# Three block seams and one loop order of a hybrid decoder step: two end-of-block transfer waits moved into the next block, the delta preparation's vector order turned round, and the first state-space quarter reordered

## The reference, cut to what matters

```
hn  = rms_norm(x) * (1 + sc1) + sh1                # modulation from c through w_ada
qkv, z, beta, alpha, u = split(hn @ w_in)
q, k, v = silu(short causal conv(qkv)); q, k normalised per head (4 heads of 128)
o   = gated delta rule(q, k, v, exp(g), beta)      # in chunks: triangular solve, then a scan
y   = S5(u)                                        # 32 groups of 16 channels, 64 complex states:
                                                   # x_t = Lbar x_{t-1} + Bbar u_t ; y = Re(C x) + D u
y   = gelu(y); y = y * sigmoid(y @ glu_w + glu_b)
x   = x + gt1 * (concat(norm(o)*silu(z), norm(y)) @ w_out)
x   = x + gt2 * moe(rms_norm(x)*(1+sc2)+sh2)       # 16 experts, top 2 within the best group of 4
out = rms_norm(x)
```

## Time and profile before

| | |
|---|---|
| median of three runs | 1240.59 us (1237.02 to 1242.99) |
| the profiled execution's own time | 1234.19 us |
| its span, first to last instruction | 1232.6 us, 15219 instructions |
| mean granted TensorE clock | 0.942 of full speed |
| TensorE matmul busy | 1077.2 us (87%) |
| VectorE busy | 553.9 us (45%) |
| ScalarE busy | 310.5 us (25%) |
| GpSimd busy | 217.5 us (18%) |
| block 1 | start to 382.2 us |
| block 2 | 382.2 to 514.8 us |
| block 3 | 514.8 to 629.9 us |
| block 4 | 629.9 us to the end |

### The profile page before, as it was taken

The page is one execution under the profiler, slowest core; times in us unless marked ns, Lnnn a source line. Parts: engine busy times, 40 slices in busy tenths (PEclk is TensorE's granted clock), DMA queues, the critical chain, the costliest instruction groups (busy, mean ns, idle before and its releaser), DMA issues. The chain is left out here.

```text
span 1232.6 us, 15219 instructions
## 1 busy us (share of the span) xinstructions
PE 1077.2 (87%) x5092; PEld 645.0 (52%) x5093; DVE 553.9 (45%) x1290; ACT 310.5 (25%) x703; POOL 217.5 (18%) x368
## 2 busy tenths in 40 slices
PE   4899999899996789499988899991999999889876
PEld 4466666445865677478763444441444444444332
DVE  3234446774355555598904424664311111111128
ACT  5122121135113443332233333321011111011033
POOL 0000000384413335100110000122210111001060
PEclk8999999999998899898988999995999999999888
DMA  9595170120016000575553100017586664788273
GB/s 345 152 292 217 68 272 1 69 103 35 14 27 139 2 1 2 164 265 188 185 193 134 69 35 19 35 46 176 167 274 223 220 223 159 266 309 287 102 290 139
DMA packets 128048, 182.02 MB, mean 148 GB/s; under 512 B 37725, under 2 KB 81490, under 8 KB 127982
## 3 DMA queue, kind: packets, MB, share of 16 engines
q1 hardware_dynamic: 116988, 147.03, 36.2%
q0 software_dynamic: 7376, 21.59, 5.4%
q10 hardware_dynamic: 3626, 12.64, 2.5%
HBM read 131.69 MB, written 48.47 MB: 146 GB/s over the span
## 5 line engine op out<-in xcount | busy, mean ns | idle before, releaser
L2163 PE MATMUL bank<-w_out,H 128*128 (+1 forms) x384 | 172.0, 601 | 10.2 <-DMA w_out<-in_w_up 5.5
L368 PE MATMUL bank<-hT,w_ring 128*128 128x344 f32 x576 | 169.7, 456 | 3.8 <-ACT hT L552 3.8
L368 PEld LDWEIGHTS bank<-hT,w_ring 128*128 128x128 f32 x576 | 109.9, 192 | 62.0 <-issue 5.4
L2163 PEld LDWEIGHTS bank<-w_out,H 128*128 128x128 f32 x384 | 72.4, 192 | 107.3 <-issue 105.4
L453 PE MATMUL bank<-w_ring,hT 128*128 128x512 f32 x256 | 114.7, 605 | 4.3 <-ACT qkvT L580 4.3
L2481 PE MATMUL bank<-w_out,hT 128*128 128x512 f32 x256 | 116.8, 601 | 0.5 <-DVE hT L1940 0.5
L2230 DVE TENSOR_TENSOR H<-H,bank 128x256 f32<-128x256 f32 x24 | 10.1, 421 | 238.2 <-ACT H L2199 238.2
L2145 PE MATMUL bank<-y1T,H 128*128 (+1 forms) x192 | 91.1, 618 | 10.7 <-DVE H L2239 7.8
L453 PEld LDWEIGHTS bank<-w_ring,hT 128*128 128x128 f32 x256 | 64.2, 255 | 50.5 <-issue 32.1
L2481 PEld LDWEIGHTS bank<-w_out,hT 128*128 128x128 f32 x256 | 46.3, 190 | 49.8 <-issue 47.2
L2145 PEld LDWEIGHTS bank<-y1T,H 128*128 128x128 f32 x192 | 35.4, 194 | 52.1 <-issue 51.7
(11 more groups left out here) (556 smaller groups left out, 1742.7 us busy)
## 6 DMA issues: line engine op xcount, KB each, us to landing
ys_d<-ZO SPq DMA_DIRECT2D x18, 1024.0 KB, 13.0
y1T<-in_w_down SPq DMA_DIRECT2D x16, 1024.0 KB, 5.4
w_out<-in_w_gate SPq DMA_DIRECT2D x16, 1024.0 KB, 8.6
w_out<-in_w_up SPq DMA_DIRECT2D x16, 1024.0 KB, 11.4
ys_d<-H ACTq DMA_DIRECT2D x24, 512.0 KB, 5.1
w_ring<-in_w_in SPq DMA_DIRECT2D x4, 2048.0 KB, 8.2
y1T<-in_w_ada SPq DMA_DIRECT2D x4, 2048.0 KB, 8.7
hT<-in_w_ada SPq DMA_DIRECT2D x4, 2048.0 KB, 13.0
```

What stands on the lines that cost most here:

```text
L368: mm = t.matmul(ps[3 * (m % 2) + s][:, 0:SEG], w_ring[:, q % 2, k, (m % 4) * P:(m % 4 + 1) * P], hT[:, k, s * SEG:(s + 1) * SEG], start=(k ...
L2163: mm = t.matmul(ps[2 + p][:, :], xT[p][:, k, :], wgu[:, bass.ds(buf, 1), k, :].rearrange("p o n -> p (o n)"), start=(k == 0), stop=(k == K ...
```

## The change

Four edits, which do not touch what is computed. The wait for the t_d and tt_d writes goes from the end of block 1 to the head of SyncE's stream in block 2. VectorE's preparation loop issues decay(c+1) behind at(c). The wait for the S5 state writes goes from the end of block 3 into VectorE's stream of block 4, behind its wait for glu_w and glu_b. And in the first quarter of block 3, GpSimd clears Vq first under a name of its own; TensorE turns V before it waits for anything, and waits for "clear" only at the modulation products; VectorE begins with table W, copies Vq behind it, and forms X0r and X0i between the tables CL and CS.

```diff
 # block 1, SyncE
                 sp.dma_start(tt_d.rearrange("p (i j) -> p i j", i=BL), Lx).then_inc(t_out, 16)
-                sp.wait_ge(t_out, 32)
 # block 2, SyncE
             def _(sp):
+                sp.wait_ge(t_out, 32)
                 for dst, src in ((Yd, tt_d), (Xd, t_d)):
 # block 2, VectorE
                 for c in range(NT):
                     b = c % 2
-                    if c + 1 < NT:
-                        decay(c + 1)
                     act.wait(v, f"egb{c}")
                     dve.did(v.tensor_copy(egl[:, c, :], egb[:, :, P - 1]), f"egl{c}")
 ...
                     dve.did(v.tensor_tensor(at_t(c), heads(ps[2 + c % 2][:, :]), D1[:, b], ALU.mult), f"at{c}")
+                    if c + 1 < NT:
+                        decay(c + 1)
 # block 3, SyncE
-                sp.wait_ge(s5_out, 64)
 # block 3, GpSimd
             def _(g):
+                pool.did(g.memset(Vq[:, :, :, :], 0.0), "Vq")
                 pool.did(g.memset(cP4[:, :, :], 0.0))
 ...
                 pool.did(g.memset(TT[:, :, :, :], 0.0))
-                pool.did(g.memset(Vq[:, :, :, :], 0.0))
                 pool.did(g.memset(zs[:, :, 0:1], 0.0), "clear")
 # block 3, TensorE (turn_inputs is split into turn_rows and turn_decode)
-                pool.wait(t, "clear")
+                turn_rows(0)
                 for q in range(4):
 ...
                     if q == 0:
-                        turn_inputs(0)
+                        turn_decode(0)
 ...
                     dve.wait(t, f"K{q}")
+                    if q == 0:
+                        pool.wait(t, "clear")
                     for c in (2 * q, 2 * q + 1):
 # block 3, VectorE
-                tt(X0r[:, :, :], X0[:, :, :], bc(LC[:, 0, :, 1], [P, GROUPS, DEC]), ALU.mult)
-                tt(X0i[:, :, :], X0[:, :, :], bc(LC[:, 1, :, 1], [P, GROUPS, DEC]), ALU.mult, "x0")
+                def decode_inputs(q):
+                    if q > 0:
+                        pe.wait(v, f"U{q - 1}")
+                    else:
+                        pool.wait(v, "Vq")
 ...
                     table(W[:, :, :, :], Wt[:, :, 0:LAGS, :], LB, Bb[:, gs, :], B2[:, gs, :], LAGS, ALU.add, f"W{q}")
+                    if q == 0:
+                        decode_inputs(0)
 ...
                     table(CL, Wt[:, :, :, :], LC, q1, q2, LAGS + 1, ALU.add, f"CL{q}")
+                    if q == 0:
+                        dve.did(v.tensor_tensor(X0r[:, :, :], X0[:, :, :], bc(LC[:, 0, :, 1], [P, GROUPS, DEC]), ALU.mult))
+                        dve.did(v.tensor_tensor(X0i[:, :, :], X0[:, :, :], bc(LC[:, 1, :, 1], [P, GROUPS, DEC]), ALU.mult), "x0")
                     table(CS, Wt[:, :, 0:LAGS, :], LC, q2, q1, LAGS, ALU.subtract, None, first=1)
-                decode_inputs(0)
                 tables(0)
 # block 4, VectorE
             v.wait_ge(g_land, 32)
+            v.wait_ge(s5_out, 64)
             for i in range(10):
```

More of the change, by code:

```diff
@@ L1616, in turn_inputs, with turn_rows, turn_decode @@
                         dve.wait(t, f"rot{q - 1}_1")
+                    turn_rows(q)
+                    turn_decode(q)
+                def turn_rows(q):
                     for x in range(NG):
-                        mm = t.transpose(ps[2 + x // 4][:, (x % 4) * P:(x % 4 + 1) * P],
-                                         V[:, q * NG + x].rearrange("p j c -> p (j c)"), ident[:, :])
+                        t.transpose(ps[2 + x // 4][:, (x % 4) * P:(x % 4 + 1) * P],
+                                    V[:, q * NG + x].rearrange("p j c -> p (j c)"), ident[:, :])
+                def turn_decode(q):
                     dve.wait(t, f"Vq{q}")
@@ L1755, in tt @@
                     dve.did(v.tensor_tensor(out, x, y, op), name)
-                tt(X0r[:, :, :], X0[:, :, :], bc(LC[:, 0, :, 1], [P, GROUPS, DEC]), ALU.mult)
-                tt(X0i[:, :, :], X0[:, :, :], bc(LC[:, 1, :, 1], [P, GROUPS, DEC]), ALU.mult, "x0")
+                def decode_inputs(q):
[3 more added lines that the diff above has]
+                        pool.wait(v, "Vq")
+                    dve.did(v.tensor_copy(Vq[:, :, LAGS - 1, :], Vd[:, q * P:(q + 1) * P].rearrange("b (g c) -> b g c", c=CH)), f"Vq{q}")
                 def tables(q):
```

## The result

The changed kernel takes 1219.75 us in the median of four runs (1217.23 to 1224.40), beside 1238.80 for the kernel before on the same chip: ratio 0.9842, interval 0.9810 to 0.9874. Six more runs in a later batch gave 0.9852 (0.9814 to 0.9890). The profiled execution took 1217.45 us, forecast 1217.2; its span fell from 1232.6 to 1215.6 us, by 17.0.

The account below looks back on a forecast made before the run. Bounds named: SyncE's write waits at block ends, a loop of waits in the preparation, and block 3's first quarter. Gains 2.6 + 9.4 + 1.2 + 3.8 = 17.0 us took 1240.6 to 1223.6, range 1214 to 1236.

Parts of the forecast that it names:

- A: Seam of blocks 1 and 2: SyncE's tt_d write wait leaves the block end, gaining 2.6 us (bounds 0 and 2.7).
- rival 1: Block ends wait for SyncE's outstanding writes anyway, so moving both write waits gives 0: 1227.4 us; chance 0.09.
- B: Delta preparation in block 2: decay(c+1) behind at(c) shortens a chunk from 4.23 to 2.94 us, gaining 9.4 (bounds 7, 10.6).
- The loop named in the prediction: Preparation: waits through R, D1, vb, the turn of v, kv, Gb and next R set the 4.23 us chunk.
- rival 2: Preparation's two-chunk loop closes in one chunk: 5.88 us instead of 4.23, losing 11.6, total 1244.6; chance 0.06.
- rival 3: Preparation: D1(c) meets GpSimd's qg(c) every chunk, period 4.2 us again, no gain there, time 1233; chance 0.05.
- the port: VectorE and GpSimd holding each other at SBUF: a 0.2 us hold, taken once each from the preparation and first-quarter gains.
- C: Seam of blocks 3 and 4: the s5_out wait leaves SyncE's block end, gaining 1.2 us (bounds 0 and 1.4).
- D: First quarter of block 3: reordered start brings the rotation 4.0 us earlier; 3.8 taken (bounds: loss 2.5, gain 5).
- Now it comes behind a long idle stretch too, so I keep 6.72: Block 3, first quarter: TensorE's stretch from CL's end to the rotation stays 6.72 us, not 12.9 at the lower clock.
- Nothing is given back there by plan: Behind the changed places, everything starts relative to its block's start, so the 17.0 us sum is kept.
- Rival 4: The gain is given back behind the blocks, for instance where expert weights arrive: some 1237 us; chance 0.05.

Follow-up runs that it names:

- a_only: Only the wait for the t_d and tt_d writes moved ahead of block 2's reads, on the kernel before: ratio 0.9993.
- b_only: Only decay(c+1) moved behind at(c) in the preparation, on the kernel before: ratio 0.9916.
- vb_last: Changed kernel with vb(c) moved behind decay(c+1), at(c) left ahead of it: 1226.63 us in one execution.
- after: The changed kernel with all four edits, in its first profile: median 1219.75 us, ratio 0.9842 to the kernel before; profiled execution 1217.45 us.
- after_again: The changed kernel run and profiled once more, unaltered: ratio 0.9852 to the kernel before.
- c_only: Only the wait for the S5 state writes moved into VectorE's block 4, on the kernel before: ratio 0.9998.
- late_e1: Changed kernel with the second expert's gate and up weights loaded behind the last h2 write: ratio 0.9804 to the kernel before.
- late_x: Changed kernel with the second expert's gate and up weights loaded behind the landing of the first gathered rows: ratio 0.9858 to the kernel before.
- vb_first: Changed kernel with decay(c+1) between vb(c) and at(c), so at(c) comes last: 1222.40 us in one execution.
- warm: Changed kernel plus unread TensorE transposes at the ends of blocks 1 and 2 and in block 3's first quarter: ratio 0.9835 to the kernel before.

## Why the prediction was right, and where its steps were off

- **A, 2.6 forecast, 2.6 measured** (3.39 to 0.78, and 0.79 in a_only). The first product starts 0.78 us behind tt_d's issue with that write still open (SyncE waits 2.2 us more for it in block 2), so a block's end did not wait for writes: rival 1 is refuted. Yd, Xd and the states were never waited for.
- **B, 9.4 forecast, 10.4 measured** (b_only 10.40; once 9.3). The loop named in the prediction was the right one, as vb_last shows with 4.16 us. The period came out at 2.9 as worked out (2.92 in the mean of after's last six but the one with the sample rows), where rival 2 asked for 5.88; rival 3 is refuted, since D1 meets qg in the first chunk alone. The missing 1.0 us was mis-sized in small terms: from at(0) to at(7) it took 20.4 us (b_only) to 20.7 (after) instead of the 20.6 + 0.7 summed, and in b_only no D1 was held, so that the 0.2 for the port fell away. The start varies: at(0) stands 5.36 us behind Gb(0) in b_only, 4.95 in after and 6.10 in after_again, where the sum had 5.28. In after_again, where the lower level lasted until 6.9 us behind tt_d's issue, B is 9.3.
- **C, 1.2 forecast, 1.3 measured** in c_only (114.14 against 115.45). VectorE's moved wait costs nothing.
- **D, 3.8 forecast, 3.5 measured**, from two errors that nearly cancel. The step that failed is "Now it comes behind a long idle stretch too, so I keep 6.72": from CL's end to the rotation it is 8.44 us, and the rotation gained 2.4 instead of 4.0 (16.50 us behind the block's start instead of 18.91; yp of quarter 0 stands at 25.7, forecast 24.3). D put K 8.1 us behind the block's start, and in none of the twelve kernels without the transposes did the level rise before 10.9 us behind it. And the output products, not in the sum, gained 1.6 us at the higher level, of which 1.1 reach the second quarter's rotation (39.52 us behind the block's start instead of 43.05). What sets the moment of the rise is not settled (10.9 to 16.2 us in those twelve), and D's size hangs on it in part: five other profiles with the same block 3 took 108.4 (late_e1) to 111.8 us (late_x) from its start to glu_b. Less C's 1.3, D is worth 2.3 to 5.7 us by these, and 3.5 is one execution's value.
- **The port.** The prediction took 0.2 us twice, from a hold that it read as shorter than the rest of qg(0). Read from the ends, it was a full one: D1(1) ends 0.55 us behind qg(0)'s end, and 0.54 to 0.56 behind it in all eight kernels where the two met, although its own time there is anything from 0.87 to 1.28 us. That is 0.14 us less than the 0.69 it takes alone; vb_first's held egl ends 0.03 behind qg, also 0.14 less than its 0.17. So the lengthening understates the hold by some 0.14 us. In D it cost nothing, since VectorE came first each time and GpSimd waited (its tiny sums took 0.57, 1.18 and 1.26 us and ended right behind VectorE's products, off the path).
- **"Nothing is given back there by plan"** held for the change and not for the numbers. Unforecast are 1.6 us of shorter kS, a recurrence of 86.3 to 92.3 us, and from glu_b's load to the end 602.2 to 608.0 us over eleven executions with the same code there but for C's wait. In the profile of after these came to +1.6, +1.7 and -3.8, tt_d was issued 0.2 later and C with D gave 4.7, so that 17.8 us of parts show as 17.0. Rival 4 saw the place, but the loss is the transfers' own spread and does not follow from the gain.
- **The range.** It was added up from narrower bounds than those stated with the parts: A from 2.3 (stated 0), C from 1 (0), D from 0 (a loss of 2.5, where its own numbers give 2.2). And B's lower bound of 7 is 3.5 below the upper bound of 10.6; 3.5 below the 9.4 taken it is 5.9. The result did not test these low ends.

## What to carry to other kernels

An instruction in one engine's order can be part of a loop over several engines: find what the others wait for in it, and issue that first (here vb, worth 10 us, more than the other three parts together). When an edit moves work towards a block's start, price TensorE's products at the lower level that the trace shows at that distance from the start (the kernel before had 0.50 until 11.0 us behind it). And do not take a sum that agrees to the tenth as proof of its terms; single-part kernels and a second profile of the same kernel told here which terms were the change's, and kernels that differed elsewhere showed how far a stretch varies on unaltered code.

## What was not expected of the hardware

Between a VectorE copy of 128x4 elements and a GpSimd product that read and wrote SBUF the second waited to the end of the first: 0.77 us instead of 0.17, ending 0.03 us behind it. The Trainium skill (SBUF — State Buffer, "Who interferes with whom") says that such a copy can enter a mode that takes the port pair shared with GpSimd, and that the later one blocks fully; the trace agrees, with the sizes above. GpSimd was held too, by VectorE's products of two SBUF inputs (0.57 to 1.26 us for its tiny sums, which took 0.20 to 0.31 in the kernel before).

The same shows in places that cost little. In the kernel before egl(7) took 0.98 us and ended 0.02 us behind qg(7). In after egl(0) took 1.98 us and ended 0.03 us behind the second of GpSimd's two memsets, which write SBUF and read nothing:

```profile
383.35 1.98 DVE L1425 COPY egl<-W 128x4 f32<-128x4 f32 x1
...
384.35 0.95 POOL L1093 MEMSET XS<- 128x1024 f32 x1
```

TensorE's granted clock falls to 0.50 for stretches of 3.4 to 20.5 us outside the routing (20.5 in a_only, from the end of block 2 to 16.2 us into block 3), in executions of the same code at different places, also where it had been at 1.00 with 2.06 of 2.80 us busy just before (warm, ahead of K). The recurrence, the same code throughout, took 86.3 us where its first 8 us ran at 1.00 (after) and 92.3 us where they ran at 0.62 (a_only).

The landing of four indirect writes of 128 numbers each varied from 7.7 us with 2 MB of loads beside them to 10.2 to 12.2 us with 4 MB.
